# Input projection with seven products: filter weights asked for a pair ahead, first filter sums ahead of token sums, late transposes in four banks

## What is computed

```python
u = _centred_conv3(h @ w_in + b_in, conv_w, conv_b)      # h: 1024 x 1024, w_in: 1024 x 3072
v, x1, x2 = jnp.split(u, 3, -1)
# filters, per order o and direction, length 1024:
h = (a @ f_w3).reshape(L, 2, HY_ORDER, D_MODEL) * window
two_sided = two_sided / jnp.sum(jnp.abs(two_sided), 0, keepdims=True)
z = x1 * long_conv(v, 0)
z = x2 * long_conv(z, 1)
```

## Time and profile before

| what | value |
|---|---|
| median of 3 runs | 3920.55 us (3915.26 to 3924.16) |
| the profiled execution, its span | 3923.02 us, 3921.2 us |
| PE, DVE, ACT, POOL busy in the span | 91%, 67%, 22%, 14% |
| the stage of the change | 57.7 to 514.3 us of the span |
| PE busy from pair 0 to the next stage (57.70 to 514.27) | 403.9 of 456.6 us |

### The profile page before, as it was taken

The page is one execution under the profiler, slowest core; times in us unless marked ns, Lnnn a source line. Parts: engine busy times, 40 slices in busy tenths (PEclk is TensorE's granted clock), DMA queues, the critical chain, the costliest instruction groups (busy, mean ns, idle before and its releaser), DMA issues. The chain is left out here.

```text
span 3921.2 us, 63593 instructions
## 1 busy us (share of the span) xinstructions
PE 3580.9 (91%) x26046; PEld 2219.4 (57%) x26046; DVE 2628.7 (67%) x3525; ACT 870.4 (22%) x1734; POOL 553.5 (14%) x559
## 2 busy tenths in 40 slices
PE   6889989997979999999999998999976998868996
PEld 2334478884445555555555555544454898535563
DVE  6667679994876767667766664454176778457773
ACT  2000012221111221221212112322135443113232
POOL 1111300002200000000000001100030876001110
PEclk9999999999989999999999999999988999988998
DMA  7553322216489999999999996212002100228996
GB/s 282 213 215 143 147 108 108 108 76 248 185 298 352 330 329 329 327 334 332 332 329 322 335 323 206 93 57 76 33 1 80 46 5 4 94 97 311 354 355 230
DMA packets 290170, 798.61 MB, mean 204 GB/s; under 512 B 18920, under 2 KB 26096, under 8 KB 275312
## 3 DMA queue, kind: packets, MB, share of 16 engines
q1 hardware_dynamic: 272048, 719.02, 50.3%
q0 software_dynamic: 17136, 73.54, 5.9%
q10 hardware_dynamic: 720, 2.17, 0.2%
HBM read 708.56 MB, written 86.11 MB: 203 GB/s over the span
## 5 line engine op out<-in xcount | busy, mean ns | idle before, releaser
L1694 PE MATMUL banks<-moe_down,moe_hidT 128*128 128x512 f32 x1280 | 565.5, 595 | 11.1 <-DMA moe_down<-d_wd 11.0
L1694 PEld LDWEIGHTS banks<-moe_down,moe_hidT 128*128 128x128 f32 x1280 | 237.4, 191 | 283.3 <-issue 277.2
L2064 PE MATMUL banks<-hT,w_in_ring 128*128 128x512 f32 (+3 forms) x976 | 364.0, 535 | 1.9 <-ACT hT L2125 1.1
L1767 ACT COPY moe_parts<-banks 128x512 f32<-128x512 f32 (+1 forms) x240 | 123.7, 515 | 837.3 <-PE banks L1673 834.3
L1673 PE MATMUL banks<-moe_wsums,moe_xsums 128*64 128x256 f32 x2560 | 298.7, 387 | 5.4 <-DVE moe_xsums L1811 4.1
L2064 PEld LDWEIGHTS banks<-hT,w_in_ring 128*128 128x128 f32 (+1 forms) x976 | 183.1, 188 | 180.9 <-issue 170.3
L1673 PEld LDWEIGHTS banks<-moe_wsums,moe_xsums 128*64 128x64 f32 x2560 | 179.7, 138 | 130.4 <-issue 46.7
L1622 POOL DMA_INDIRECT moe_xe<-d_xhat,chosen x32 | 50.4, 1575 | 1133.2 <-PE banks L1666 1040.9
L901 PE MATMUL banks<-x_block,dft 128*128 128x256 f32 x896 | 196.7, 382 | 5.9 <-PEq L399 5.9
L901 PEld LDWEIGHTS banks<-x_block,dft 128*128 128x128 f32 x896 | 171.7, 192 | 30.0 <-issue 6.3
L1673 PE MATMUL banks<-x_block,moe_xeT 128*64 128x256 f32 x1536 | 183.1, 381 | 0.0
(11 more groups left out here) (494 smaller groups left out, 6360.8 us busy)
## 6 DMA issues: line engine op xcount, KB each, us to landing
moe_down<-d_wd SPq DMA_DIRECT2D x160, 1024.0 KB, 11.2
x_block<-d_wg SPq DMA_DIRECT2D x96, 1024.0 KB, 6.8
x_block<-d_wu SPq DMA_DIRECT2D x96, 1024.0 KB, 9.0
mix<-d_wg SPq DMA_DIRECT2D x64, 1024.0 KB, 8.7
mix<-d_wu SPq DMA_DIRECT2D x64, 1024.0 KB, 11.4
x_block<-d_seq SPq DMA_DIRECT2D x19, 1024.0 KB, 4.8
w_in_ring<-d_w_in SPq DMA_DIRECT2D x9, 2048.0 KB, 10.2
x_block<-d_mod_w SPq DMA_DIRECT2D x16, 1024.0 KB, 6.4
```

The costliest lines, as they stand in the source:

```text
L1694: last = nc.tensor.matmul(m.ps[:, Y_BANK + h, :], hidT[:, j % 2, i * P:(i + 1) * P], wd[:, i, h * BANK:(h + 1) * BANK], start=(fc == 0 and ...
L1767: nc.scalar.copy(pp[:, to, :], m.ps[:, bank, 0:w * HN].rearrange("p (a n) -> p a n", a=w)).then_inc(s.copied, 1)
L2064: last = nc.tensor.matmul(m.ps[0:width, g % 6, 0:n], ring[:, q % 2, k, at:at + width], hT[:, k, first:first + n], start=(k == 0), stop=(k ...
```

## The change

Three edits, all in this stage.

1. `load_filter` is split. The weights of block n+2 are now asked for at the top of SP's loop of pair n, behind a wait for `sum_diff(n)`, which has read the buffer that they overwrite (`s.w3pq`). The bias stays behind the store of the taps. In the setup the bias of block 0 moves behind the second weight chunk.
2. On DVE, `sum_diff(0)` stands ahead of the token sums instead of behind them.
3. The transposes of the last four pairs (8 to 11, turned in pairs 9 to 11 and after) use four banks in turn instead of one: bank 4, the two banks of the filter products, which are done by then, and the bank of the matrix times vector rows.

```diff
+def load_filter_weights(sp, m, j):
     b, w3 = j % 2, filter_weights(m)
     for a in range(2):
         sp.dma_start(w3[a * FW:(a + 1) * FW, b], m.dram["f_w3"][:, :, j * Q:(j + 1) * Q]).then_inc(...)
+def load_filter_bias(sp, m, j):
+    b = j % 2
     sp.dma_start(m.f_bias[:, b, :], m.dram["f_bias"][:, j * Q:(j + 1) * Q]).then_inc(...)
...
             load_input_chunk(sp, m, 0, 0)
-            load_filter(sp, m, 0)
+            load_filter_weights(sp, m, 0)
             load_window(sp, m, 0)
             load_input_chunk(sp, m, 0, 1)
-            load_filter(sp, m, 1)
+            load_filter_bias(sp, m, 0)
+            load_filter_weights(sp, m, 1)
+            load_filter_bias(sp, m, 1)
...
-        SUM_BANKS, TURN_BANK = (0, 1, 5), 4
+        SUM_BANKS, TURN_BANKS = (0, 1, 5), (4, GEN_BANK, GEN_BANK + 1, ROW_BANK)
+        turn_bank = lambda n, i, par: TURN_BANKS[2 * i + par if n >= N_IT else 0]
...
             for n in range(PAIRS_IN):
+                if n + 2 < N_IT:
+                    sp.wait_ge(s.w3pq, 2 * (n + 1))
+                    load_filter_weights(sp, m, n + 2)
                 next_mv(n, 0)
                 next_mv(n, 1)
                 if 1 <= n <= N_IT:
...
                     if j + 2 < N_IT:
-                        load_filter(sp, m, j + 2)
+                        load_filter_bias(sp, m, j + 2)
...
                 pe.wait_ge(s.conv, unit + 1)
-                if g:
+                if n >= N_IT:
+                    pe.wait_ge(s.staged, max(g - 3, 4 * N_IT))
+                elif g:
                     pe.wait_ge(s.staged, g)
+                if n == N_IT and g == 4 * N_IT:
+                    pe.wait_ge(s.gen_read, 8 * N_IT)
...
+            sum_diff(0)
             nc.vector.tensor_tensor(t3[:], b22, b12, ALU.subtract).then_inc(s.token_sums, 1)
...
             gen = Steps(v, s.pair)
-            sum_diff(0)
```

More of the change, by code:

```diff
@@ L175, in filter_weights @@
     return early[:, 4 * TT * Q:4 * TT * Q + 4 * Q].rearrange("p (s d c) -> p s d c", s=2, d=2)
-def load_filter(sp, m, j):
+def load_filter_weights(sp, m, j):
     b, w3 = j % 2, filter_weights(m)
@@ L520, in turn @@
                 pe.wait_ge(s.conv, unit + 1)
-                if g:
+                if n >= N_IT:
+                    pe.wait_ge(s.staged, max(g - 3, 4 * N_IT))
+                elif g:
                     pe.wait_ge(s.staged, g)
+                if n == N_IT and g == 4 * N_IT:
+                    pe.wait_ge(s.gen_read, 8 * N_IT)
                 for j in range(4):
                     last = nc.tensor.transpose(
-                        m.ps[:, TURN_BANK, j * P:(j + 1) * P],
+                        m.ps[:, turn_bank(n, i, par), j * P:(j + 1) * P],
                         uc[:, i, 4 * P * (j % 2) + 2 * par + j // 2:4 * P * (j % 2 + 1):4], m.ident[:])
@@ L650, in _, with sum_diff @@
             w_at, b_at = COLS["conv_w"][0], COLS["conv_b"][0]
+            def sum_diff(j):
+                v.wait_ge(w3_in[j % 2], 32 * (j // 2 + 1))
+                nc.vector.tensor_tensor(w3pq[:, 0, :], w3[:, j % 2, 0, :], w3[:, j % 2, 1, :], ALU.add).then_inc(s.w3pq, 1)
+                nc.vector.tensor_tensor(w3pq[:, 1, :], w3[:, j % 2, 0, :], w3[:, j % 2, 1, :], ALU.subtract).then_inc(s.w3pq, 1)
+            sum_diff(0)
             nc.vector.tensor_tensor(t3[:], b22, b12, ALU.subtract).then_inc(s.token_sums, 1)
@@ L668, in collect @@
                     stage[:, n % 2, 4 * par:4 * par + 4, i * P:(i + 1) * P],
[L669 to L674, removed]
+                    m.ps[:, turn_bank(n, i, par), :].rearrange("p (j c) -> p j c", c=P)).then_inc(s.staged, 1)
             def windowed(g):
```

## The result

The changed kernel takes 3871.7 us (median of 4 runs, 3867.39 to 3872.39), the kernel before 3921.24 us (median of 4, 3915.26 to 3924.16). The ratio is 0.9873, with a 95% interval of 0.9856 to 0.989: 49.5 us less. The profiled execution of the changed kernel took 3871.78 us, with a span of 3870.0, against 3923.02 and 3921.2.

What follows compares the result with a forecast made beforehand. TensorE, 91% busy, was taken as the bound, its gaps caused by filter weights queued behind a 2 MB store. Gains 36.8 + 5.2 + 3.5 = 45.5 us gave 3877.5 from the profiled 3923.02, 3875 by median, range 3866 to 3888.

Steps and rivals of the forecast that it cites:

- The weights: Pairs 2 to 7: earlier request ends DVE's waits for filter weights; 40.2 us less losses of 2.0 and 1.4, gain 36.8.
- The floor: Pairs 2 to 7: TensorE's own work, 215.4 us of the 255.55, so at most 40.2 us to be had.
- The window: Pairs 2 to 5: the next late load, there at 9.7 to 10.3 us, costing TensorE 0.5 us a pair, 2.0 in all.
- I take 1.0, an estimate: Pairs 2 to 5: microseconds the window comes earlier without the weights in front, between nothing and 2.7.
- 1 to 2 us in pairs 2 to 5: Sign expected in the profile: DVE waits this long for the window there, and not in pairs 6 and 7.
- The slack of 1.5 us: At TensorE's second transpose in a pair: DVE's lateness of up to 1.5 us from the window would be covered.
- The seam: Where pairs meet, POOL's sums beside DVE: a 0.9 us surcharge, covered by the window's wait in pairs 2 to 5.
- my estimate of 3 us: Pair's seam under the skill's lockout rule: some 3 us a pair; pairs 6 and 7 would lose up to 2 each.
- The first sums: Pair 0: second filter step at 74.5 instead of 79.68; gain 5.2 us, bounds 3.5 and 6.9.
- The four banks: Stage's end: late quarters no longer wait for one bank; gain 3.5 us, bounds 2.0 and 4.4.
- the clock came back: Rival, 6%, said it would not: 8 to 10 us of slow products stay or go elsewhere; gain 36, 3885 us.
- the last rival: Slower, 2%: the moved request holds SP 20.72 us, slots come late, TensorE waits 9.4 us in six pairs: 3931 us.

Runs made afterwards that it cites:

- the kernel with two banks: Changed kernel with DVE's stage start reordered, plus transposes of pairs 5 to 7 in two banks in turn instead of one: 3863.34 us, ratio 0.9846.
- The kernel with `bias_diff` moved: Changed kernel with `bias_diff` right behind `sum_diff(0)` and the last two token sums behind the first window products: 3864.58 us, ratio 0.9861.

## Why the prediction held, and where it did not

The forecast was 3875.0 us and 3871.7 was measured, inside 3866 to 3888. The mechanism is as it was put, and its three terms are these.

**The weights: 36.8 us forecast, 40.0 measured.** The floor was too high. I took 37.68 us for pairs 2 and 4 and 33.79 for pairs 6 and 7. TensorE's own time is 37.00 where pair 2 has no gaps, and 33.29 and 32.50 in pairs 6 and 7 of the kernel with two banks, the only one in which they have none. With 37.00 twice, 36.21 twice, 33.29 and 32.50 the floor is 212.2, and 43.3 us were to be had, not 40.2. The busy time of a pair with gaps holds work made longer by them, and not at a lower clock alone: pair 2 had its 37.68 at a granted clock of 1.00. The losses were 3.3 us where I had 3.4, but this agreement is luck. Pairs 2 to 5 lost 0.8 in place of 2.0, all of it in pair 3, and pairs 6 and 7 lost 2.5 (1.26 and 1.25) in place of 1.4.

**The window.** "I take 1.0, an estimate" was too little. The windows of pairs 2 to 5 landed 11.0, 12.2, 11.1 and 11.1 us after their requests, against 12.8, 13.4, 13.0 and 12.7 before, so they came 1.2 to 1.9 us earlier. DVE's waits were 1.33 us in pair 3, 0.17 in pair 4 and 0.19 in pair 5, not "1 to 2 us in pairs 2 to 5". The slack of 1.5 us was too large. The wait of 1.33 us made pair 3 0.8 us longer than a pair without gaps, 0.25 of it at the second transpose, and with the window behind the chunk 5.98 us made pair 2 5.4 us longer. In both cases only 0.5 us was covered. That the window came earlier than I took it to made up for this.

**The seam.** Here I chose the wrong price. I took 0.9 us from one convolution step. The two sums took 2.63 us in place of the 0.83 that they take with POOL held back, and the first step of the second convolution 1.16 in place of 0.80 (in the other pairs up to 1.36): together some 2.2 us at the seam. The rule of the Trainium skill (SBUF — State Buffer, Who interferes with whom) is that a DVE instruction with two SBUF inputs and a GpSimd instruction that reads SBUF lock each other out for a whole instruction. The trace agrees: POOL's two weight sums end at 129.93 and 131.35, and the two sums of DVE end 0.3 us behind each. A meeting thus costs what is left of the POOL operation, and my estimate of 3 us, a whole operation for each, was above the measured 2.2, but nearer than 0.9.

What the surcharge costs in time, no run isolates. In pairs 2 and 4, 37.00 us without a gap, it costs nothing. In pair 6 DVE works without a wait from its filter sums at 276.31 to the collection at 295.52, and TensorE waits 0.68 us for this collection; the surcharge ahead of it is longer than the wait. So it is the likely cause of the 2.5 us that pairs 6 and 7 lost, for which I had put down up to 2 us each by that rule. A second bank takes the wait away. This is read from the order of the rows and not shown by a run.

**The first sums: 5.2 us forecast, 3.5 measured**, the low bound, which had named the lower clock. The step that failed is not the order on DVE. The second filter step came 5.9 us earlier than in the earlier trace rows, 5.15 without the 0.7 by which the stage began earlier, as worked out. But I left a gap of 3 us in front of it (3.06 with this edit alone, 2.20 behind the wait for the slot) and priced what follows at full speed. The filter step took 2.03 us in place of 1.25 and the product 4.58 in place of 3.70: 1.7 us given back at the lower clock. The kernel with `bias_diff` moved has no gap, and there the two take 1.25 and 3.70.

**The four banks: 3.5 us forecast, 3.8 measured.** The last copy ended at 461.1, 5.2 us ahead of the next stage's first product at 466.3; before it was 509.1 and 514.3, also 5.2. So what stands behind the last copy followed it, as the forecast had it.

**The sum.** In the stage 47.3 us were won where 45.5 were forecast. The terms were off by +3.2, -1.7 and +0.3, so their errors cancel in part. Of the 3.3 us between the forecast and the measured time these are 1.8; the rest lies outside the stage.

**The rivals.** The store was what stood in the weights' way, and the clock came back: 1.00 in pairs 2 to 7. SP was held by the moved request, as the last rival had it, but for 5.48 us where the same request took 1.21 before, and under the 19 us from which it would have decided. The slots were then asked for 9.3 us into pair 2, earlier than the 11.4 of before.

## What to carry to other kernels

When an engine waits for a small load, read what was asked for ahead of it in the same queue: a store that nobody waits for can stand in front of it, and a place a few lines higher gives nearly all that a long lead gives. Take the floor of a loop from an iteration without gaps, since the busy time of one with gaps is too high, even at full clock. Where a gap before TensorE is made shorter but not closed, price what stands behind it at the lower clock, and see whether the last piece of it can go too.

## What the runs showed of the hardware

- DVE and POOL each held the other up. Two sums of 0.42 us took 1.15 and 1.48 while POOL added weights, and were short again when POOL waited. The convolution's steps of 1.29 then took 2.2, and POOL's own 1.29 became 1.70. While both were at it, each DVE sum ended 0.3 us behind a sum of POOL.
- A request can hold its queue's engine by itself: the same two requests, 128 KB each, took SP 1.2 us in the old place and 5.48 just behind the 2 MB chunk.
- A gap of 2.2 to 3.1 us on TensorE made the next twelve instructions 1.7 us longer in all (6.6 us in place of 4.95), at a mean granted clock of 0.73 in place of 1.00.
- A window of 1 MB landed in 11.0 us when 256 KB of weights no longer stood between it and the 2 MB store, and in 12.8 when they did. With the weights ahead of both it landed in 11.6.
